# The opening of a two-layer hybrid trunk: scale products, shift products and the first weight split in another order

## What is computed

```python
sh1, sc1, g1, sh2, sc2, g2 = jnp.split((jax.nn.silu(c) @ mod_w[l] + mod_b[l])[:, None, :], 6, axis=-1)
csh1, csc1, cg1, csh2, csc2, cg2 = jnp.split(jax.nn.silu(c_ctx) @ mod_w[l] + mod_b[l], 6)
h = modulate(rms_norm(x, norm1_g[l]), sh1, sc1)        # h * (1 + scale) + shift
hc = modulate(rms_norm(cx, norm1_g[l]), csh1, csc1)
...
q, k, v, glu = jnp.split(h @ w_in, cuts, axis=-1)       # in even_mixer
attn = dense_block_attention(q, ...)
conv = conv_module(glu, dw_w, dw_b, cn_g, cn_b)         # a * sigmoid(gate), 31-tap convolution
```

## Time and profile before

| | us |
|---|---|
| Median of the runs shown (lowest, highest) | 1195.97 (1194.71, 1196.26) |
| The profiled execution | 1194.39 |
| Its span | 1192.6 |
| PE busy in it | 1153.7 |
| DVE busy in it | 692.7 |
| ACT busy in it | 486.0 |
| POOL busy in it | 9.8 |
| First product of the first weight block starts | 25.76 |
| Fifth slice of block 2 starts | 68.00 |

### The profile page before, as it was taken

One profiled execution on the slowest core, in us unless ns is written; L12 is line 12 of the kernel. 1 busy time (PEld: TensorE's weight loads), 2 busy tenths in 40 slices (PEclk: granted clock), 3 DMA queues, 4 the chain that ended last, 5 costly groups with the idle time before them and its releaser, 6 DMA issues.

```text
span 1192.6 us, 17704 instructions
## 1 busy us (share of the span) xinstructions
PE 1153.7 (97%) x7238; PEld 933.8 (78%) x7238; DVE 692.7 (58%) x1160; ACT 486.0 (41%) x744; POOL 9.8 (1%) x18
## 2 busy tenths in 40 slices
PE   5999999999999999999999999999999999999998
PEld 4767776777688888888887767899565798998997
DVE  5489987854443324333323358887789645554455
ACT  4233235643333332222222333367268635443442
POOL 1000000000000000000000000000000000000000
PEclk9999999999999999999999999999999999999999
DMA  9745655025553222333223564244130157655551
GB/s 346 276 142 164 209 204 176 1 66 217 176 177 106 69 72 86 126 109 103 79 80 106 194 217 132 82 140 143 36 127 17 37 179 245 210 178 176 188 171 66
DMA packets 118893, 167.73 MB, mean 141 GB/s; under 512 B 4797, under 2 KB 102695, under 8 KB 114599
## 3 DMA queue, kind: packets, MB, share of 16 engines
q1 hardware_dynamic: 118390, 166.23, 41.8%
q10 hardware_dynamic: 433, 0.51, 0.2%
HBM read 164.37 MB, written 1.05 MB: 139 GB/s over the span
## 4 chain that ended last, share of the span: by engine, by line
PE 86%; DVE 9%; ACT 3%; issue 1%; DMA 1%; SPq 0%; DVEq 0%; ACTq 0%; POOL 0%
PE acc L2138 20%; PE acc L2139 20%; PE acc L2140 20%; PE pmod L2061 2%; PE acc L2222 2%; PE acc L2223 1%; PE acc L2224 1%; PE p L2509 1%; PE p L2507 1%; PE p L2508 1%; PE acc L1998 1%; PE p L1998 1%; DVE Y L1420 1%; DVE sm L1503 1%; DVE w_lo L644 1%
## 5 line engine op out<-in xcount | busy, mean ns | idle before, releaser
L644 DVE TENSOR_TENSOR w_lo<-raw,w_hi 128x1024 fp32r<-128x1024 f32 x222 | 249.0, 1162 | 235.3 <-ACT w_hi L634 235.0
L634 ACT ACTIVATE w_hi<-raw 128x1024 fp32r<-128x1024 f32 (+1 forms) x224 | 212.9, 999 | 408.0 <-PE acc L2140 358.1
L2138 PE MATMUL acc<-Hhi,w_hi 128*128 128x512 f32 (+1 forms) x960 | 326.3, 340 | 4.5 <-DVE w_lo L644 3.9
L2140 PE MATMUL acc<-Hhi,w_lo 128*128 128x512 f32 (+1 forms) x960 | 324.3, 338 | 0.0
L2139 PE MATMUL acc<-Hlo,w_hi 128*128 128x512 f32 (+1 forms) x960 | 324.3, 338 | 0.0
L2138 PEld LDWEIGHTS acc<-Hhi,w_hi 128*128 128x128 f32 x960 | 182.1, 190 | 29.2 <-issue 5.9
L2140 PEld LDWEIGHTS acc<-Hhi,w_lo 128*128 128x128 f32 x960 | 182.1, 190 | 19.6
L2139 PEld LDWEIGHTS acc<-Hlo,w_hi 128*128 128x128 f32 x960 | 182.1, 190 | 19.1
L2138 PE MATMUL acc<-hid_hi,w_hi 128*128 128x512 f32 x248 | 97.9, 395 | 0.1
L2139 PE MATMUL acc<-hid_lo,w_hi 128*128 128x512 f32 x248 | 96.6, 390 | 0.0
L2140 PE MATMUL acc<-hid_hi,w_lo 128*128 128x512 f32 x248 | 96.6, 389 | 0.0
(11 more groups left out here) (387 smaller groups left out, 1593.9 us busy)
## 6 DMA issues: line engine op xcount, KB each, us to landing
raw<-in_mod_w SPq DMA_DIRECT2D x44, 1024.0 KB, 5.2
raw<-in_ffn_w_in SPq DMA_DIRECT2D x44, 1024.0 KB, 5.1
raw<-in_od_w_in SPq DMA_DIRECT2D x15, 1024.0 KB, 5.3
raw<-in_ffn_w_out SPq DMA_DIRECT2D x12, 768.0 KB, 4.5
raw<-in_ev_w_in SPq DMA_DIRECT2D x8, 1024.0 KB, 7.5
raw<-in_od_w_out SPq DMA_DIRECT2D x8, 1024.0 KB, 6.4
raw<-in_ffn_w_out SPq DMA_DIRECT2D x8, 1024.0 KB, 5.0
raw<-in_ev_w_out SPq DMA_DIRECT2D x8, 768.0 KB, 6.0
```

What stands on the lines that cost most here:

```text
L634: nc.scalar.activation(w_hi[:, w % 2, c0:c1], raw[:, r % RAW_SLOTS, c0:c1], ACT.Copy)\
L644: nc.vector.tensor_tensor(w_lo[:, w % 2, c0:c1], raw[:, r % RAW_SLOTS, c0:c1], w_hi[:, w % 2, c0:c1].bitcast(F32), ALU.subtract).then_inc( ...
L2138: mm(outs[m], hi[:, j, cols], xh, start=(first and j == 0), stop=False)
L2140: ins = mm(outs[m], lo[:, j, cols], xh, start=False, stop=(last and j == kts - 1))
```

## The change

Six things move.
- SP: the first half of weight block 0 is loaded ahead of the first two scale transfers instead of behind them. Further on the transfer of block 2 stands ahead of that of `mod_unit` 8. The semaphores of the scale transfers are told apart (`scales_loaded0` for units 0 and 1, one each for units 2 and 3).
- POOL: part 0 of block 0 is split by POOL, both halves of it, behind its two squares. ACT's `first_hi(0, 0)` and DVE's `first_lo(0, 0)` go.
- PE: unit 1 stands behind all sums of squares. Units 2 and 3 come ahead of the first weight products. Units 4 to 7 stand together between the first and the second half of the pair of blocks. `shift_T` stands inside block 0's second half, the shift products ahead of block 1's second half, and `bias_columns` between its two output tiles.
- PE waits for DVE's own count (`h_lo_dve`) for slices 0 and 1.
- DVE: the first `scales_copy` stands behind the reciprocal, the second between `gained0` 2 and 3, `first_gains(1)` ahead of the split of part 1. Block 2 is split whole ahead of `first_bias`.
- ACT: a one-element sigmoid is added ahead of the wait for the bias.

```diff
@@ -346,7 +346,9 @@
-            if 1 <= n <= 8:
+            if n == 2:
+                stream.append(("mod", 0, 1, 0))
+            if 2 <= n <= 8:
                 stream.append(("mod", 0, 1, n - 1))
@@ -484,9 +486,9 @@
+            first_block(0, 0, s("first_rows0"))
             first_scales(0)
             first_scales(1)
-            first_block(0, 0, s("first_rows0"))
             first_block(1, 0, s("first_rows1"))
@@ -695,6 +697,12 @@
+            pool.wait_ge(s("first_rows0"), 16)
+            nc.gpsimd.tensor_copy(w_hi[:, 0, 0:1024], raw[:, 0, 0:1024]).then_inc(hi_split, 1)
+            pool.wait_ge(hi_split, 1)
+            nc.gpsimd.tensor_tensor(w_lo[:, 0, 0:1024], raw[:, 0, 0:1024], w_hi[:, 0, 0:1024].bitcast(F32), ALU.subtract)\
+                .then_inc(lo_split, 1)
@@ -782,9 +790,9 @@
-            first_hi(0, 0)
             first_high(0)
             first_high(1)
+            act.wait_ge(hi_split, 1)
             first_hi(1, 0)
@@ -821,6 +829,7 @@
                 if n == 0:
+                    step(A(sm[:, 0, 7:8], epsc[:, 0:1], ACT.Sigmoid))
                     act.wait_ge(s("bias_ready"), 1)
@@ -1355,11 +1364,10 @@
-            scales_copy(0)
             dve.wait_ge(s("rt_ready"), 1)
             V_.reciprocal(rs0[:, :], rt0[:, :]).then_inc(s("rs_ready"), 1)
+            scales_copy(0)
             first_gains(0)
-            first_lo(0, 0)
@@ -1381,13 +1389,14 @@
+            scales_copy(1)
             gained0(3)
+            dve.wait_ge(lo_split, 1)
             first_lo(1, 0)
             low0(3)
+            first_gains(1)
             first_lo(0, 1)
             first_lo(1, 1)
-            scales_copy(1)
-            first_gains(1)
@@ -1465,10 +1474,9 @@
-                    split(2, parts=(0,))
+                    split(2)
                     first_bias()
                     shifted_low(range(4, KD))
-                    split(2, parts=(1,))
@@ -2108,10 +2116,13 @@
             for f in range(KD):
                 first_sum(f)
-                if f in (3, 5):
-                    mod_unit(f // 4)
+                if f == 3:
+                    mod_unit(0)
+            mod_unit(1)
             scales_T(0)
             spread_roots(0, T)
+            mod_unit(2)
+            mod_unit(3)
@@ -2172,38 +2183,33 @@
                 for j in range(4):
+                    pe.wait_ge(s("h_lo_dve") if j < 2 else s("h_lo"), j + 1)
+                    if j == 3:
+                        scales_T(1)
+                    for m in range(2):
+                        column(0, j, m)
+                pe.wait_ge(lo_split, FIRST[1, 0])
+                for j in range(4):
+                    for m in range(2):
+                        ins = column(1, j, m)
+                ins.then_inc(s("h_used"), 1)
+                for m in range(4, KD):
+                    mod_unit(m)
...
                 pe.wait_ge(lo_split, FIRST[1, 1])
                 pe.wait_ge(s("shift_ready"), 1)
                 shift_product(0).then_inc(block_done, 1)
                 shift_product(1).then_inc(s("bias_rows"), 1)
                 for j in range(4, KD):
-                    if j == 6:
-                        bias_columns()
+                    column(1, j, 0)
+                bias_columns()
+                for j in range(4, KD):
                     ins = column(1, j, 1)
```

More of the change, by code:

```diff
@@ L478, in first_scales @@
                 sp.dma_start(first_mod[i][:, :].rearrange("p (k n) -> p k n", k=4),
-                             tiles(a["mod_w"][0, rows_:rows_ + 4 * P, cols_:cols_ + 4 * P])).then_inc(s(f"scales_loaded{i // 2}"), 16)
+                             tiles(a["mod_w"][0, rows_:rows_ + 4 * P, cols_:cols_ + 4 * P])).then_inc(s(f"scales_loaded{max(i - 1, 0)}"), 16)
             def first_block(r, part, loaded):
@@ L2018, in mod_unit @@
                 if m < 4:
-                    pe.wait_ge(s(f"scales_loaded{m // 2}"), 32)
+                    pe.wait_ge(s(f"scales_loaded{max(m - 1, 0)}"), 32 if m < 2 else 16)
                     if m == 0:
@@ L2174, in first_two @@
                 for j in range(4):
+                    pe.wait_ge(s("h_lo_dve") if j < 2 else s("h_lo"), j + 1)
[10 more added lines that the diff above has]
+                    mod_unit(m)
+                pe.wait_ge(lo_split, FIRST[0, 1])
+                for j in range(4, KD):
+                    if j == 6:
+                        shift_T()
                     pe.wait_ge(s("h_lo"), j + 1)
@@ L2177, in first_two @@
                         column(0, j, m)
[L2178 to L2195, removed]
                 pe.wait_ge(lo_split, FIRST[1, 1])
-                for j in range(4, KD):
-                    if j == 6:
-                        shift_T()
-                    column(1, j, 0)
                 pe.wait_ge(s("shift_ready"), 1)
```

## The result

| us | before | after |
|---|---|---|
| Median of 4 runs each | 1195.34 | 1188.03 |
| Lowest, highest | 1194.09, 1196.26 | 1187.63, 1188.53 |
| The profiled execution, and its span | 1194.39, 1192.6 | 1188.06, 1186.3 |
| First weight product starts | 25.76 | 27.26 |
| Fifth slice of block 2 starts | 68.00 | 62.88 |

The ratio is 0.994, with an interval from 0.9923 to 0.9957. The change wins 7.3 us, the forecast said 3.7, and 1188.03 lies under the range of 1190.0 to 1195.0. The sign was right and the size was not.

What follows compares the result with a forecast made beforehand. PE, busy 1153.7 of 1192.6 us, was taken as the bound. First product 27.0 + 35.8 kept work + waits 0.9 and 0.6 = 64.3 against 68.00, 3.7 us less: forecast 1192.3, range 1190.0 to 1195.0.

Steps and rivals of the forecast that it cites:

- the low clock (my 1.6): PE's first weight products run at 1.2 GHz after 2.75 us idle; the change removes this, worth 1.6 us.
- the new waits (my 0.9 and 0.6): PE would newly wait 0.9 us before slice 3 and 0.6 us for unit 7's data.
- The first product (my 27.0): PE's first weight product would start at 27.0 instead of 25.76, late by 1.2 us.
- So data isn't the last: Unit 3's data land at 25.5, PE is free at 26.5, so data would not decide the first product at 27.0.
- The collision on DVE's squares: POOL's cast and subtraction would hold up DVE's squares by the port lock; the last squares end at 21.0, formerly 18.5.
- both late waits: PE's waits at block 2's start, 0.61 us, and before its fifth slice, 2.36 us, would both go.
- 35.8: Time PE keeps from first weight product to block 2's fifth slice, without waits, units 2 and 3 and low clock.
- 42.24: The distance before, from PE's first weight product at 25.76 to block 2's fifth slice at 68.00, in us.
- No collision: Rival: POOL and DVE do not collide at the squares; gain 5.0 us, 1191.0; chance 0.24.
- The clock falls nonetheless: Rival: PE's clock still falls in the opening, costing 1.6 us; gain 2.1, 1193.9; chance 0.11.
- Slower: Rival: POOL's two instructions at 15.45 last much longer than expected, up to 2.4 us slower, 1198.4; chance 0.05.
- DVE not forward: Rival: DVE starts the later blocks no earlier, leaving about 0.5 of the gain, 1195.5; chance 0.07.

Runs made afterwards that it cites:

- kernel 6: Kernel before plus two unused 128x128 by 512-column products ahead of the first weight product, filling PE's idle gap; 1193.17 us, ratio 0.9985.
- execution of 1193.0: One of two more profiled executions of the kernel before, unchanged; 1193.0 us.
- execution of 1195.98: The other of two more profiled executions of the kernel before, unchanged; 1195.98 us.
- kernel 2: Changed kernel with POOL's split undone, so ACT and DVE split part 0 of block 0 again; 1187.11 us, ratio 0.9934.
- kernel 11: kernel 7 with ACT's `Hhi` of slice 2 and DVE's `Hlo` of slice 3 each ahead of block 1's split; 1185.67 us, ratio 0.9928.
- kernel 7: Changed kernel with POOL's split held until DVE's squares are done, and scale and half-block transfers reordered; 1188.13 us, ratio 0.9945.
- kernel 4: Kernel before with the two late edits alone: sigmoid table load ahead of the bias wait, block 2 split whole ahead of the bias; 1191.08 us, ratio 0.9967.
- kernel 8: Kernel before with only the middle: units 4 to 7 together, shift and bias products in the new order; 1192.44 us, ratio 0.9984.
- kernel 9: Changed kernel with the middle and late edits undone, leaving only the opening; 1192.42 us, ratio 0.9979.
- kernel 1: Changed kernel with units 2 and 3 back behind block 0's first four slices, their copy and gains too; 1190.01 us, ratio 0.9958.
- kernel 5: Kernel before, unchanged, 11 runs; 1195.73 us, ratio 1.0006.
- kernel 10: Kernel before, unchanged, profiled twice more; 1195.98 and 1193.0 us.

## Why the prediction was wrong

**The size, split.** From the first product to the columns behind units 2 and 3 kernel 6 takes 7.97 at full clock. The profile of the earlier trace rows takes 9.11, the execution of 1193.0 takes 8.96 and that of 1195.98 takes 10.20: 1.1, 1.0 and 2.2 of low clock. The execution of 1193.0 has no other stretch, so without it before would take about 1192.0, a worked-out figure; the lowest runs of kernel 6, at 0.999 and 1.000, were 1192.1. Against 1188.03 that leaves 4.0 for the structure. The median of before beside after, 1195.34, lies 3.3 above the same mark: that is low clock. After has none in its profile, and its four runs have a mean clock of 0.999 to 1.000. So of the 7.3 some 4.0 are structure and 3.3 are clock.

**The failed step: the low clock (my 1.6).** The mechanism was right, the size was off by two. I priced one stretch from one execution as if it were a constant. The median execution of before holds 3.3 us of it: the opening single or prolonged, and in some executions another stretch behind the wait of 2.36. The one stretch that I did price is worth only 1.1 in time, since at full clock PE waits for slice 3; 1.6 was what its products cost.

By places, 3.6 are missing. Ahead of the fifth slice it is 1.4 (68.00 to 62.88 is 5.1, and I had 3.7). Behind it, it is 1.2, of which 0.9 is the stretch at 316 us, which after lacks. It stood in the trace that I had, but the change can't reach that work, so I never looked there. The last 0.95 is how far the profiled execution lay under the median of 1195.34. In the forecast that distance was 1.6 (1195.97 less 1194.39), and I carried it over as a plain offset; the execution of 1195.98 shows what it was, low clock in the opening and near 69 that the change removes. Had I asked why 1195.97 is above 1194.39, it would have been in the sum.

**The failed step: the new waits (my 0.9 and 0.6).** Measured are 0.24 and none. For slice 3 I added DVE's copy of 0.28 to the row. It stands there, at 28.24, but it delays only the split behind it, which POOL's `Hlo` (28.55 to 29.84) held anyway: POOL passed slice 3 on at 31.59, 4.65 after the first `Hlo` was done at 26.94, not 5.05. Here the instruction that was added in front of a held one cost nothing. Also PE came there later than I said (31.5, not 31.1), since it started at 27.26. And the wait isn't new: kernel 6 has 0.25 of it in the old order. For unit 7 the issue came at 34.90, exactly as worked out, but landed in 6.8, not 7.6: two rows of the trace after.

```profile
34.90 0.37 SPq L517 DMA_DIRECT2D raw<-in_mod_w  x1
```

```profile
raw<-in_mod_w SPq DMA_DIRECT2D x1, 1024.0 KB, 6.8
```

That is 41.7, and PE wants unit 7 only near 41.8. Kernels 2 and 11, where PE comes there earlier, wait 0.26 and 0.16 for that transfer. A landing time read once isn't good to 0.6 us; I should have kept it in the range with zero at its other end. Both together are 1.3.

**The first product (my 27.0).** It came at 27.26, but the context's data had started to move 0.7 later than in the trace of before (other executions scatter over some tenths as well). Counted from the data, it is 0.8 late, not 1.2. Step by step the numbers were met: squares done at 21.03 (21.0), reciprocal 22.19 (21.95), spread 23.50 (23.4), first `Hlo` 26.94 (26.9). That is partly luck. POOL's second square ends at 16.10 instead of 15.40, so the chain should have come 0.7 later throughout; the collision took as much less than I reckoned. POOL's subtraction, which lasts 2.35 by itself (kernel 7) and not 2.56, made up 0.3 of it, and DVE's second square, which lost 0.2 (0.88 for 0.68) and not 0.4, most of the rest. The step that failed is "So data isn't the last": unit 3 waits 0.68 for its data, and its end, not `Hlo`, releases the product.

**Right.** The collision on DVE's squares, the cast (1.04), the table load out of the way, both late waits gone, DVE earlier: its first work behind block 2's slices starts at 62.09, against 67.8. The blocks keep the gain; the earlier trace rows reads almost alike after:

```profile
70.00:160.00 90.00, 90.00 (x536) 70.39 (x535) 89.48 (x127) 26.46 (x27) 0.00 (x0) 1.00 0.56 187
```

With the measured terms: 27.26 + 35.8 + 0.24 = 63.3; it was 62.88. Most of the last 0.4 lies in what I took from 42.24. A pause cost a little more than the idle time in its bracket: from unit 8 to block 2 it is 1.67 before (60.95 to 62.62) and 0.99 after (59.03 to 60.02), 0.68 for the 0.61, and from the fourth to the fifth slice 3.20 (64.80 to 68.00) and 0.68 (62.20 to 62.88), 2.52 for the 2.36. The low clock's product work was 1.7 (7.23 for 24 products, 5.5 at 0.23).

**The rivals.** "No collision" fell. Kernel 2 is the nearest to it, though it lacks POOL's split altogether: 0.5 to 0.9 more, where I had said 1.3. "The clock falls nonetheless" fell: the first products are 0.23 apart at clock 1.00, and PE's longest pause from 23 on is 0.75. "Slower" fell, and so did "DVE not forward", though kernel 4 shows 0.9 of it for the late edits alone. No rival held a gain over 5.7, because all of them shared the single price of the clock.

**The parts don't add up.** Kernels 4, 8 and 9 alone win 4.7, 2.3 and 2.0, in all 9.0, and the whole 7.3. The middle and the late part both claim the wait of 2.36 and what the clock loses behind it, so whichever comes first gets it. That is the plain reading; no run splits the 1.7 between them.

**Left open.** Why the clock falls at a place in one execution and not in another of the same kernel, with the same waits in front of it (kernels 1, 5 and 10), above all at 316 us. Kernel 9's profile has the pause of 2.37 and no fall behind it. That it depends on when the pause comes is likely and isn't shown. Nor is it shown why kernel 2 is faster than after when unit 3's data come last in both; the earlier start of the data explains 0.4 of it.

## What to carry to other kernels

Before you price a low clock, look for every stretch of it in the trace and ask how far the profiled execution lies from the median, for that distance can be clock too: a pause of 2 to 3 us that sometimes makes it fall costs its own length plus, on the average, part of the slow work behind it, and slow work that hides another wait costs less time than it takes (here 1.1 for 1.7). Where two engines share ports, the one that starts first wins, so look at the order of starts to a tenth of a us (26.87 against 26.97 in kernel 7), and put the instruction that others wait for first on both engines. And a wait that follows from the difference of two long sums (here 0.9 and 0.6 us) is uncertain by as much as it is long: it belongs in the range before it belongs in the sum.

## What the runs showed of the hardware

- The lock between DVE and POOL works both ways. DVE lost at 18.16 (2.87 for two squares of 0.64) and in the split at 29.22 (1.71 instead of 1.22); POOL lost in kernel 7 (2.85 instead of 1.29). The Trainium skill (SBUF — State Buffer, Who interferes with whom) says that whoever issues first blocks the other wholly, and by these rows that holds for POOL as the loser too, which the trace of before did not show.
- Size doesn't protect: in kernel 7 DVE's gain on 128 x 8, with both inputs in SBUF, took 0.74 instead of 0.17 while POOL subtracted.
- POOL casts 1024 columns of fp32 in 1.04 and subtracts 1024 in 2.35 uncontended (2.70 in the change, where DVE's square, 16.75 to 17.63, was ahead of it). The Trainium skill (GPSIMD Engine Reference, Engine selection) puts one-input work near line rate, and the cast agrees: ACT's rounding of as many columns takes 1.04 as well, and POOL's own square of half as many, with two inputs, also 1.04.
- The same program, with the same waits in each of its profiles, ran from 1193.0 to 1196.4 us, nearly in the order of its mean granted clock (0.999 to 0.996).
